# Linear attention by heads in another order, and the first and last microseconds of a two-block transformer kernel rewritten

## The reference

```python
def rmsnorm(x, g):
    y = x * lax.rsqrt(jnp.mean(x * x, axis=-1, keepdims=True) + NORM_EPS)
    return y * g

# first step of the program: a gated feed-forward layer on the normed input
x = x + 0.5 * swiglu(rmsnorm(x, norm_gains[0, 0]), ffn_w_in[0, 0], ffn_w_out[0, 0])
...
# gated linear attention (4 heads, keys of 128, values of 256), over chunks of 64
def step(S, xs):
    qc, kc, vc, gc = xs
    b = jnp.cumsum(gc, axis=1)
    q_dec = qc * jnp.exp(b)
    k_inv = kc * jnp.exp(-b)
    A = jnp.where(lower, einsum('bqhd,bkhd->bhqk', q_dec, k_inv), 0.0)
    o = einsum('bhqk,bkhv->bqhv', A, vc) + einsum('bqhd,bhdv->bqhv', q_dec, S)
    b_last = b[:, -1]
    k_end = kc * jnp.exp(b_last[:, None] - b)
    S = jnp.exp(b_last)[..., None] * S + einsum('bkhd,bkhv->bhdv', k_end, vc)
    return S, o
# run forwards and backwards in time; o = rms_norm(o_f + o_b) * silu(out_gate); y = o @ w_o
...
# last step of the program
f_lat = jnp.square(jax.nn.relu(modulate(x_lat, ...) @ w_mlp_in[1])) @ w_mlp_out[1]
x_lat = x_lat + m_lat[5] * rms_norm(f_lat, g_post_mlp[1])
```

## Time and profile before

| | us |
|---|---|
| median of 3 runs | 2374.57 |
| lowest, highest | 2373.31, 2375.43 |
| the profiled execution | 2382.3 |
| its span | 2381.0 |
| PE busy | 2254.7 (95%) |
| DVE busy | 1209.8 (51%) |
| ACT busy | 981.1 (41%) |
| POOL busy | 499.9 (21%) |

### The profile page before, as it was taken

One profiled execution on the slowest core, in us unless ns is written; L12 is line 12 of the kernel. 1 busy time (PEld: TensorE's weight loads), 2 busy tenths in 40 slices (PEclk: granted clock), 3 DMA queues, 4 the chain that ended last, 5 costly groups with the idle time before them and its releaser, 6 DMA issues.

```text
span 2381.0 us, 37755 instructions
## 1 busy us (share of the span) xinstructions
PE 2254.7 (95%) x16663; PEld 2052.4 (86%) x16663; DVE 1209.8 (51%) x1463; ACT 981.1 (41%) x1179; POOL 499.9 (21%) x447
## 2 busy tenths in 40 slices
PE   6999899998999999899999999999999999888998
PEld 6999898878999999667999976888888897577997
DVE  5655565666555555466655356352222273545434
ACT  4433344444443443354444356443322244534442
POOL 2211344331221220221222211011211301221220
PEclk8999999999999999899999999999999999888998
DMA  6555443354555555598554410132323232114551
GB/s 243 171 179 174 142 141 124 123 187 164 185 169 191 175 190 170 196 328 297 177 184 170 133 36 19 36 124 89 101 94 97 99 119 89 54 54 143 189 181 54
DMA packets 205245, 344.72 MB, mean 145 GB/s; under 512 B 8845, under 2 KB 69498, under 8 KB 205082
## 3 DMA queue, kind: packets, MB, share of 16 engines
q1 hardware_dynamic: 205082, 342.31, 43.2%
HBM read 341.24 MB, written 1.05 MB: 144 GB/s over the span
## 4 chain that ended last, share of the span: by engine, by line
PE 83%; DVE 7%; POOL 4%; ACT 3%; issue 2%; DMA 1%; SPq 0%; DVEq 0%; POOLq 0%; ACTq 0%
PE PS L474 79%; PE PS L483 3%; DVE WL L460 2%; POOL small L1527 1%; ACT WH L444 1%; DVE XL L642 1%; POOL TMP L1536 1%; POOL small L1525 1%; DVE TMP L1453 1%; DMA raw<-in_b_w_out 0%; POOL TMP L1537 0%; DVE small L1431 0%; DVE TMP L1458 0%; DVE al L3084 0%; POOL TMP L2757 0%
## 5 line engine op out<-in xcount | busy, mean ns | idle before, releaser
L460 DVE TENSOR_TENSOR WL<-raw,WH 128x2048 fp32r<-128x2048 f32 (+2 forms) x281 | 652.0, 2331 | 678.2 <-ACT WH L444 678.2
L474 PE MATMUL PS<-XH,WH 128*128 128x256 f32 (+1 forms) x2368 | 700.6, 296 | 21.0 <-DVE WL L460 11.0
L474 PE MATMUL PS<-XL,WH 128*128 128x256 f32 (+1 forms) x2368 | 697.5, 295 | 0.0
L474 PE MATMUL PS<-XH,WL 128*128 128x256 f32 (+1 forms) x2368 | 697.3, 294 | 0.0
L444 ACT ACTIVATE WH<-raw 128x2048 fp32r<-128x2048 f32 (+2 forms) x281 | 519.5, 1859 | 357.1 <-PE PS L474 355.8
L474 PEld LDWEIGHTS PS<-XH,WH 128*128 128x128 f32 x2368 | 457.7, 193 | 33.3 <-DVE WL L460 12.1
L474 PEld LDWEIGHTS PS<-XL,WH 128*128 128x128 f32 x2368 | 457.6, 193 | 8.8
L474 PEld LDWEIGHTS PS<-XH,WL 128*128 128x128 f32 x2368 | 457.4, 193 | 8.7
L474 PE MATMUL PS<-WH,XH 128*128 128x256 f32 (+2 forms) x944 | 288.6, 306 | 14.2 <-DVE XL L642 6.0
L474 PE MATMUL PS<-WL,XH 128*128 128x256 f32 (+2 forms) x944 | 280.4, 297 | 0.0
L474 PE MATMUL PS<-WH,XL 128*128 128x256 f32 (+2 forms) x944 | 280.0, 297 | 0.0
(11 more groups left out here) (250 smaller groups left out, 2501.1 us busy)
## 6 DMA issues: line engine op xcount, KB each, us to landing
raw<-in_ffn_w_in SPq DMA_DIRECT2D x88, 1024.0 KB, 5.1
raw<-in_w_mod SPq DMA_DIRECT2D x48, 1024.0 KB, 6.2
raw<-in_ffn_w_out SPq DMA_DIRECT2D x40, 1024.0 KB, 5.0
raw<-in_a_w_in SPq DMA_DIRECT2D x36, 1024.0 KB, 5.0
raw<-in_w_mlp_in SPq DMA_DIRECT2D x32, 1024.0 KB, 5.5
raw<-in_w_mlp_out SPq DMA_DIRECT2D x32, 1024.0 KB, 5.0
raw<-in_gla_w_in SPq DMA_DIRECT2D x12, 1024.0 KB, 5.2
raw<-in_attn_w_qkv SPq DMA_DIRECT2D x6, 1024.0 KB, 5.1
```

The source lines that it names most:

```text
L460: dve.e.tensor_tensor(self.WL[j % NRAW][:, 0:nk * nn], self.raw[j % NRAW][:, 0:nk * nn], wh.bitcast(F32), ALU.subtract).then_inc(*self.lo. ...
L474: return self.pe.e.matmul(out, l, r, start=start, stop=stop, skip_group_check=skip)
```

## The change

Three places are rewritten; the arithmetic stays the same but for the last norm.

- **Start.** SP issues weight chunk 0 directly behind `x`, ahead of the rows, and chunks 1 to 5 directly behind the rows. PE transposes three pairs of `x` before it waits for the rows. ACT splits chunk 0 and squares the first half of `R` before it makes `XH`, and squares the second half behind it; POOL only folds, and only once `XL` is complete. DVE splits chunk 0 before it makes `XL`.
- **Linear attention.** PE computes `result(h)` before it turns the next head's keys. ACT copies the turned keys behind the squares of the result, and the logarithm for head h + 2 moves behind these copies. DVE spreads the next head's steps between the states of this head.
- **End.** The last norm is applied by tokens. `R` is turned to tokens early: 12 transposes behind the attention's output layer, 4 inside the first chunk pair of the last MLP, with four copies (two ACT, two DVE) into `eR`. The layer's result times the gain (`eY`) is turned by PE, the first half of it (8 transposes) inside the second half of the last linear layer. The sum of squares is made as single columns (2 early, 8 behind the layer), so root and reciprocal are 128x2, and one DVE instruction per 128x512 piece multiplies and adds; it is stored right after.

```diff
-FIRST = 3
+FIRST = 6
...
+        self.eR = v(self.r_at, 0, [128, 2048]).rearrange("p (b d) -> p b d", b=2)
+        self.eY = self.tiles(v(self.tmp_at, 0, [128, 2048]))
...
-        self.finish_pe()
...
+        self.load_weights(0)
...
-        for c in range(FIRST):
+        for c in range(1, FIRST):
...
-            self.feed_pool("f0", q, [(self.r_act, (1, 2 * q)), (self.r_dve, (1, 2 * q + 1))], [])
+            pool.wait_ge(self.xl, ("f0", 7))
+            pool.wait_ge(self.sq_act, ("f0", q))
+            self.pool_fold(self.first_squares(q), ("f0", q))
...
     def start_pe(self):
         pe = self.pe
+        pe.wait_ge(self.ld_ident, "ident")
+        pe.wait_ge(self.ld_x, "x")
+        self.residual_pe(1, range(3))
         pe.wait_ge(self.ld_rows, "rows")
-        pe.wait_ge(self.ld_ident, "ident")
         for i, n in enumerate(self.SIZES):
             self.tr(self.PS[:, 4 + i, 0:n], self.rows[0:n, i, :], n).then_inc(*self.turned.up(("rows", i)))
             self.empties([4 + i], (self.col, i))
-        pe.wait_ge(self.ld_x, "x")
-        self.residual_pe(1)
-
+        self.residual_pe(1, [3])
+
...
+    def first_squares(self, q):
+        return self.tiles(self.TMP[:, 2048:4096])[:, 4 * q:4 * q + 4, :]
+
     def start_act(self):
-        self.residual_act(1)
         for q in range(2):
+            self.residual_act(1, [2 * q])
+            if q == 0:
+                self.act_part()
+                self.squares_first(q)
             self.feed_act("f0", q, 0, 0, [(self.r_act, (1, 2 * q)), (self.r_dve, (1, 2 * q + 1))], [])
+        self.squares_first(1)
+
+    def squares_first(self, q):
+        act = self.act
+        act.wait_ge(self.r_act, (1, 2 * q))
+        act.wait_ge(self.r_dve, (1, 2 * q + 1))
+        act.e.activation(self.first_squares(q), self.R[:, 1, 4 * q:4 * q + 4, :], ACT.Square).then_inc(*self.sq_act.up(("f0", q)))
 
     def start_dve(self):
         dve, at = self.dve, 0
+        self.residual_dve(1, [1])
         for i, n in enumerate(self.SIZES):
             dve.wait_ge(self.turned, ("rows", i))
             dve.e.tensor_copy(self.COL[:, at:at + n], self.PS[:, 4 + i, 0:n]).then_inc(*self.col.up(i))
             at += n
         self.col.name("all")
-        self.residual_dve(1)
+        self.dve_part()
         for q in range(2):
+            if q:
+                self.residual_dve(1, [3])
             self.feed_dve("f0", q, 0, 0, [(self.r_act, (1, 2 * q)), (self.r_dve, (1, 2 * q + 1))], [])
...
+            self.turn_r_pe(t, self.END_R[:3])
+
+    END_R = [(0, 0, 6), (0, 1, 7), (1, 0, 4), (1, 1, 5)]
+
+    def turn_r_pe(self, t, parts):
+
+        pe = self.pe
+        for q, tb, b in parts:
+            pe.wait_ge(self.res, (t, 1, q))
+            self.pe_bank(b)
+            for k in range(4):
+                m = self.tr(self.PS[:, b, k * 128:k * 128 + 128], self.R[:, 1, 4 * q + k, tb * 128:tb * 128 + 128])
+            m.then_inc(*self.turned.up(("end r", q, tb)))
+            self.empties([b], (self.evac, ("end r", tb)) if q == 0 else (self.emptied, ("end r", tb)))
+
+    def turn_r_act(self):
+        for tb in range(2):
+            self.act.wait_ge(self.turned, ("end r", 0, tb))
+            self.act.e.activation(self.eR[:, tb, 0:512], self.PS[:, 6 + tb, :], ACT.Copy).then_inc(*self.evac.up(("end r", tb)))
+
+    def turn_r_dve(self, tb):
+        self.dve.wait_ge(self.turned, ("end r", 1, tb))
+        self.dve.e.tensor_copy(self.eR[:, tb, 512:1024], self.PS[:, 4 + tb, :]).then_inc(*self.emptied.up(("end r", tb)))
...
+                    self.pe_linear(w_in[:, c0:c0 + 512], xs, b0, T, name, mid=(lambda: self.turn_r_pe("gla", self.END_R[3:])) if first else None, tiles=first)
...
-            next(fill)
+            for _ in fill:
+                pass
             if h < 2:
                 gates(h + 2)
+            result(h)
             if h < 3:
                 for d in range(2):
                     turn_keys(h + 1, d)
-            next(fill)
-            result(h)
-            for _ in fill:
-                pass
...
             act.e.activation(a, a, ACT.Exp, scale=-1.0).then_inc(*self.a_step.up(("gla", "exp", h)))
+            yield
...
                 pass
-            if h < 3:
-                for d in range(2):
-                    turn_keys(h + 1, d)
             act.wait_ge(self.lin, ("gla", "g", h))
             act.e.activation(self.gG[:, :, h * 256:h * 256 + 256], PS[:, 7, :].rearrange("p (b d) -> p b d", b=2), ACT.Silu).then_inc(*self.evac.up(("gla", "g", h)))
             ahead = gates(h + 2) if h < 2 else iter(())
             next(ahead, None)
             result(h)
+            if h < 3:
+                for d in range(2):
+                    turn_keys(h + 1, d)
+            next(ahead, None)
...
                 next(ahead)
-            else:
-                for _ in range(3):
-                    next(ahead, None)
             for d in range(2):
                 masked(h, d)
                 state(h, d, 0)
                 state(h, d, 1)
-                if h == 0 and d == 0:
-                    for _ in range(3):
-                        next(ahead)
+                next(ahead, None)
             for d in range(2):
                 state(h, d, 2)
                 state(h, d, 3)
+                next(ahead, None)
             for _ in ahead:
                 pass
...
+    def turn_y_pe(self, q):
+
         pe = self.pe
+        for tb in range(2):
+            b = 4 * q + tb
+            self.pe_bank(b)
+            for k in range(4):
+                pe.wait_ge(self.gated_, ("end", q, k // 2 if q else 0))
+                m = self.tr(self.PS[:, b, k * 128:k * 128 + 128], self.eY[:, 4 * q + k, tb * 128:tb * 128 + 128])
+            m.then_inc(*self.turned.up(("end", q, tb)))
+
+    def closing_pe(self, src, xs):
+        pe = self.pe
+        SQ = self.tiles(self.TMP[:, 2048:4096])
+
+        def column(k, tb, first, last):
+
+            m = self.mm(self.PS[:, 2 + tb, 0:1], SQ[:, k, tb * 128:tb * 128 + 128], self.ONES[:, 0:1], first, last, True)
+            if last:
+                m.then_inc(*self.summed.up(("end", tb)))
+
+        def early():
+            self.turn_y_pe(0)
+            for tb in range(2):
+                self.pe_bank(2 + tb)
+                pe.wait_ge(self.sq, ("mlp1", 0, 1))
+                column(0, tb, True, False)
+
+        for half in range(2):
+            self.pe_linear(src[:, half * 512:half * 512 + 512], xs, 4 * half, 256, ("mlp1", "o", half), mid=early if half else None)
+            self.empties(range(4 * half, 4 * half + 4), (self.y_dve, ("mlp1", half, 1)))
+        for i in range(2):
+            pe.wait_ge(self.sq_act, ("mlp1", 1, i))
+            for tb in range(2):
+                for k in (4 + 2 * i, 5 + 2 * i):
+                    column(k, tb, False, k == 7)
+        self.turn_y_pe(1)
+
+    def closing_act(self, free):
+        act = self.act
+        SQ = self.tiles(self.TMP[:, 2048:4096])
+        self.act_begin(4)
+        self.to_y_act(("mlp1", 0, 1), 0, 1, None, None, False, True, free)
+        self.act_begin(4)
+        for i in range(2):
+            k = 4 + 2 * i
+            act.wait_ge(self.y_dve, ("mlp1", 1, i))
+            act.e.activation(SQ[:, k:k + 2, :], self.Y[:, 1, k:k + 2, :], ACT.Square).then_inc(*self.sq_act.up(("mlp1", 1, i)))
+        rs = self.small[:, 0:2]
+        act.wait_ge(self.summed, ("end", 1))
+        act.e.activation(rs.unsqueeze(2), self.PS[:, 2:4, 0:1], ACT.Sqrt, scale=1.0 / D, bias=self.MH[:, 8:9]).then_inc(*self.root.up("end"))
+
+    def closing_dve(self, before):
+        dve, PS = self.dve, self.PS
+        gain = self.MA[:, 1, 3, :, 0]
+        Y, out = self.Y[:, 1], self.eR
+
+        def gated(k, n, ready, key):
+            dve.wait_ge(*ready)
+            dve.e.tensor_tensor(self.eY[:, k:k + n, :], Y[:, k:k + n, :], gain[:, k:k + n].unsqueeze(2).to_broadcast([128, n, 256]), ALU.mult).then_inc(*self.gated_.up(key))
+
+        self.dve_begin(4)
+        self.to_y_dve(("mlp1", 0, 1), 0, 1, PS[:, 0:4, 0:256], ("mlp1", "o", 0), before(0, 1))
+        dve.wait_ge(self.mod, (1, 11))
+        dve.wait_ge(self.hl, ("mlp", 1, 1, 3))
+        gated(0, 4, (self.y_dve, ("mlp1", 0, 1)), ("end", 0, 0))
+        self.dve_begin(4)
+        dve.wait_ge(self.lin, ("mlp1", "o", 1))
+        dve.wait_ge(*before(1, 1))
+        for i in range(2):
+            k = 4 + 2 * i
+            dve.e.tensor_tensor(Y[:, k:k + 2, :], PS[:, k:k + 2, 0:256], Y[:, k:k + 2, :], ALU.add).then_inc(*self.y_dve.up(("mlp1", 1, i)))
+        self.y_dve.name(("mlp1", 1, 1))
+        for i in range(2):
+            gated(4 + 2 * i, 2, (self.y_dve, ("mlp1", 1, i)), ("end", 1, i))
+        rs = self.small[:, 0:2]
+        dve.wait_ge(self.root, "end")
+        dve.e.reciprocal(rs, rs).then_inc(*self.rstd_.up("end"))
+        dve.wait_ge(self.rstd_, "end")
+        dve.wait_ge(self.evac, ("end r", 1))
         for q in range(2):
             for tb in range(2):
```

(9 more changed lines are left out.)

51 lines of the change are left out of this document (18 added, 33 removed).

## The result

| | before | after |
|---|---|---|
| median of the runs, us | 2375.0 (4) | 2353.4 (4) |
| lowest, highest | 2373.3, 2376.6 | 2347.9, 2356.7 |
| the profiled execution, its span | 2382.3, 2381.0 | 2356.4, 2354.8 |

The ratio is 0.9905 (95% interval 0.9889 to 0.992): faster by 21.6 us, where 34.7 were forecast and 2332 was the low, 2348 the high end of the range. The direction held, the size didn't. Repeated runs give, all together, 12 executions of the changed kernel from 2347.1 to 2356.7 with a median of 2350.6, and 51 of the kernel before from 2372.0 to 2382.5 with a median of 2375.7, so the gain is about 25 us. Taken set by set, each against the runs of before beside it, the ratios are 0.9905, 0.9873 and 0.9883, gains of 21.6, 31.5 and 28.6 us. In every case it falls short.

What follows compares the result with a forecast made beforehand. PE, working 95% of the span, was taken as the bound. Start 9.7, linear attention 16.4, into the last MLP -0.5 and end 9.1 sum to 34.7; 2374.6 - 34.7 = 2339.9 us, range 2332 to 2348.

Steps and rivals of the forecast that it cites:

- start: Start of the kernel: first matmul at 13.4 instead of 23.8, chunk 1 done at 28.3 instead of 38.0; 9.7 us gained.
- attention: Linear attention: three PE stalls on DVE's state copies and the half clock behind them go, less new waits; 16.4 us gained.
- to the last big matmul: Last MLP and last layer: four transposes cost 0.5 us, extra transposes and columns less one all-ones product cost 1.0.
- behind it: Tail from the last big matmul to the span's end: 8.8 us instead of 18.9, 10.1 gained.
- The half clock behind them goes too: Linear attention: PE's stretches at 1.2 GHz behind the three stalls (11.0, 6.9, 6.5 us) return to full clock, +11.8 us.
- 3.5 for one new stretch: Linear attention, head 0: the clock falls behind the 2.7 us wait, some 7 us at half, -3.5 (bounds 0 and -5.2).
- 2.7 for backward states: Linear attention, head 0: PE waits 2.7 us for DVE's last backward states (from 0 to 4.4).
- 1.2 for each of three key copies: Linear attention, heads 1 to 3: scores wait 1.2 us each for ACT's copy of turned keys, -3.6 (0 to 3.0 each).
- ACT becomes the bound: Linear attention rival, chance 0.15 whole or in part: key waits 3.0 instead of 1.2, clock falls behind two; 2351.7 us.
- Rows at the bound of 10.9: Start: rows of gains were taken to land at 9.2, or 10.9 if behind all of chunk 0's data; then about 8.5 gained.
- 0 of "0 to 0.5": Start: cost of POOL's folds beside DVE's split of chunk 1, bounded at 0 to 0.5 us and taken as 0.
- two rivals with 0.15 and 0.06: Attention: ACT becomes the bound (0.15, 2351.7); the stall only moves, so only start and end gain (0.06, 2356.3).

Runs made afterwards that it cites:

- both_a: Changed kernel with ACT's exponential behind the key copies, rows issued first by ACT, all x pairs turned and copied before them, R's second squares behind chunk 1's split: 2342.7 us.

## Where the prediction was right and wrong

By stage, the gain of each trace of the changed kernel on the trace of before, in us. (The lead of the same PE instruction at the stage's end less that at its start.)

| stage | forecast | first trace | second | third |
|---|---|---|---|---|
| start | 9.7 | 7.8 | 5.9 | 4.8 |
| 226 to 1976 us, not changed | 0 | -2.9 | +2.0 | +2.0 |
| attention | 16.4 | 9.2 | 15.0 | 12.1 |
| to the last big matmul | -1.5 | +2.0 | +2.2 | +2.4 |
| behind it | 10.1 | 10.1 | 10.1 | 10.0 |
| sum | 34.7 | 26.2 | 35.2 | 31.3 |

The same three traces against the second trace of before:

| stage | forecast | first trace | second | third |
|---|---|---|---|---|
| start | 9.7 | 7.0 | 5.1 | 4.0 |
| 226 to 1976 us, not changed | 0 | -4.1 | +0.8 | +0.7 |
| attention | 16.4 | 9.2 | 15.0 | 12.0 |
| to the last big matmul | -1.5 | -3.6 | -3.3 | -3.1 |
| behind it | 10.1 | 8.5 | 8.5 | 8.4 |
| sum | 34.7 | 17.0 | 26.0 | 22.1 |

In the mean of the six columns the attention is 4.3 short of its term and the start 3.9. These are the two steps that failed; the others are within 1 us. (In the first two traces 1.6 of the attention's gain lies ahead of the window shown above, where nothing was changed.)

- **Attention, the clock: the largest error.** The step is "The half clock behind them goes too", +11.8, less 3.5 for one new stretch. In the first trace the attention's granted clock stayed at 0.87 and PE was busy 84.5 us instead of 84.9, so of the 8.3 net hardly anything came; in the other two the clock rose to 0.94 and 0.92 and 6.1 and 4.8 us came. The same waits of 2.0, 2.35 and 3.43 were followed by different stretches of half clock: behind the last of them the clock was 0.84 over 40.7 us in the first trace, 0.95 over 36.5 in the second. The bounds of the term (0 and -5.2) covered one wait, where three could bring the clock down.
- **Attention, the waits: nearly right in sum, wrong in place.** Forecast 2.7 for backward states, 0.6, and 1.2 for each of three key copies, 6.9 in all; measured 2.0, and 2.35 and 3.43 for two: 7.8. The rival "ACT becomes the bound" had the mechanism. It put three heads where only two have `gates(h + 2)` ahead of the copies; behind head 2 the wait is zero. The step that mis-sized it: the 1.2 counts ACT's own instructions ahead of the copies and not what they wait for. ACT's absolute value waits for POOL, and POOL was nowhere in this part of the sum. In the trace of before POOL's products lay ahead of the split; DVE's spread moved them beside it.
- **Start: 1.9 short in the first trace, 3.8 and 4.9 in the others.** Rows at the bound of 10.9 instead of 9.2: first matmul 14.5 for 13.4. The fold beside the split of chunk 1: 3.4 instead of 2.29, and the wait 1.67 instead of 0.4. The value taken was 0 of "0 to 0.5"; the rule of the Trainium skill (SBUF — State Buffer, section "SBUF: two separate sides") that the later of the two waits for the other, weighed there as up to 1.3, was right: the split took 1.1 longer. The clock rose at 19.1, as taken. The column sums of the second and third trace came at 33.0 and 34.2: there the clock fell behind the waits for chunk 1 (1.9 and 2.3), so that its 48 products took 7.5 instead of 6.0, and in the third `x` landed 1.3 later (7.4).
- **The sums of 35.2 and 31.3 agree by luck.** The trace of before that the sum was made against is 9.2 us slower than its second one, and 5.5 of these lie on the way to the last big matmul, where the forecast has a loss of 1.5 and no gain. Only 1.6 of them, in the tail, are in a term of the sum; start and attention are as short against either trace. So the base didn't make the forecast too high (with the second trace's tail the sum would be 33.1). It made the changed kernel's traces look better: 26.2 in the first, 21.6 by the medians.
- **Handover and end.** The wait ahead of the last MLP is 2.4 for 3.7, as the transposes fill it. Whether they cost nothing can't be told: the stage gains 2 us on one trace of before and loses over 3 on the other, and the forecast's -1.5 lies between. The tail behind the last matmul was forecast at 8.8 and is 8.8 to 8.9 in all three traces, term by term.
- **The range** left out 2353 because it is narrower than what its own terms allow. Its low ends for start (8.4), attention (8), handover (-0.5) and end (8) add up to 23.9, which is 2350.7, and two rivals with 0.15 and 0.06 stood at 2351.7 and 2356.3, while only a tenth was given to all that lies above 2348.
- **Two slips that change nothing in the sum.** The 3.7 ahead of the last MLP is not the third longest wait within reach: those for the rows (8.4) and for the tail's `R` (6.2) are longer, and are counted with start and end. And 5.8 us at 0.215 are 27 products, not 25.

The best version, `both_a`, keeps all of the change and moves five things; its gain over it is shown by non-overlapping times, and its parts by the traces. What remains open is whether the parts alone add up to less than the whole, and what in the attention decides whether a wait is followed by half clock.

## What to carry to other kernels

Take two traces of the kernel before and compare by stage: a total that agrees with one of them may owe it to a stretch that the sum never counted. A stall that goes is worth its length, less the waits that follow it (here 15.0 us of stalls left 7.8 of others); the half clock behind it is only a chance. When a step moves on one engine, look at what it now lies beside on the engine that shares its memory access: here DVE's split and POOL's products lengthened each other by 1 to 2 us, and each such microsecond reached PE where PE was waiting for that chain, and none where there was time to spare (`both_a`). And in an in-order list, what matters of an instruction is what the ones ahead of it wait for: one line moved on ACT took 5.8 us of waits away, of which 2.2 came back on DVE.

## What the runs showed of the hardware

- DVE's two-input split and POOL's products hold each other up for the whole of the other's length: each ends as if it had begun only at the other's end (the split took 3.35 for 2.29, products 2.77 for 0.73 and 3.31 for 1.27). A one-input DVE copy of 128x2048, 1.22 with POOL idle, blocks POOL and is blocked by it as well.
- The small rows, issued behind 2 MB or more of other transfers, landed at 11.0 to 11.2 with the last issued by SP at 6.4 (12.3 where `x` itself came 1.3 late) and at 10.4 to 10.9 with the last issued by ACT at 5.5 to 6.0; before, with 1 MB ahead of them and the last issued at 5.8, at 8.4.
- In the kernel before, 1.5 us more of PE's work at half clock ahead of a stall shortened the stall by 1.5 and left the stretch at 27.9 us.
- The granted clock behind the same waits, in the same kernel, was 0.87, 0.94 and 0.92 over the attention, and executions of one kernel differ by up to 10 us (2372.0 to 2382.5) with it.
